# First projections of an RWKV block: seven block products in place of eight

## The reference, cut to what matters

```
h = rms_norm(x, l0_norm)
dx = token_shift(h) - h                 # token t-1 minus token t
x_r, x_w, x_k, x_v, x_a, x_g = (h + dx * mu[i] for i in range(6))
r = x_r @ w_in[:, c[0]:c[1]]            # 1024 x 1024 weights each
k = x_k @ w_in[:, c[1]:c[2]]
v = x_v @ w_in[:, c[2]:c[3]]
g = silu(x_g @ w_in[:, c[3]:c[4]])
w_lo = tanh(x_w @ w_in[:, c[4]:c[5]])   # 64 columns
a_lo = x_a @ w_in[:, c[5]:c[6]]         # 64 columns
kk = k * k_k
```

## Time and profile before

| | us |
|---|---|
| median of 3 runs | 3114.89 (3111.95 to 3125.24) |
| span of the profiled execution | 3120.0 |
| first and last start of a matmul of line 331 | 39.7 and 754.3 |
| matmuls of the projection stage | 3072 |

### The profile page before, as it was taken

One profiled execution on the slowest core, in us unless ns is written; L12 is line 12 of the kernel. 1 busy time (PEld: TensorE's weight loads), 2 busy tenths in 40 slices (PEclk: granted clock), 3 DMA queues, 4 the chain that ended last, 5 costly groups with the idle time before them and its releaser, 6 DMA issues. The chain is left out here.

```text
span 3120.0 us, 78648 instructions
## 1 busy us (share of the span) xinstructions
PE 2897.5 (93%) x35058; PEld 2391.3 (77%) x35058; DVE 1605.3 (51%) x2628; ACT 1080.2 (35%) x2001; POOL 619.7 (20%) x417
## 2 busy tenths in 40 slices
PE   7999999999878888888889999999999999999899
PEld 4887888887467787777777778888777897777677
DVE  5533242433177677677764662222377204777762
ACT  4223332322635445454453441000222113556310
POOL 5522222210023232232321120000000001332320
PEclk9999999999979899899998999999999999999999
DMA  5123331211833232332316763111111226225472
GB/s 173 61 78 115 108 105 48 95 48 53 260 103 112 64 105 77 92 106 70 105 37 179 223 180 74 34 41 41 41 61 61 88 89 229 74 88 181 154 245 85
DMA packets 344272, 326.20 MB, mean 105 GB/s; under 512 B 14159, under 2 KB 258255, under 8 KB 343296
## 3 DMA queue, kind: packets, MB, share of 16 engines
q1 hardware_dynamic: 315344, 261.72, 27.6%
q10 hardware_dynamic: 24480, 47.21, 4.3%
q0 software_dynamic: 4112, 12.25, 1.5%
HBM read 203.18 MB, written 122.64 MB: 104 GB/s over the span
## 5 line engine op out<-in xcount | busy, mean ns | idle before, releaser
L331 PE MATMUL pj_ps<-pj_x_hi,pj_w_hi 128*128 128x512 f32 x1024 | 402.1, 393 | 10.6 <-DVE pj_w_lo L280 5.8
L331 PE MATMUL pj_ps<-pj_x_hi,pj_w_lo 128*128 128x512 f32 x1024 | 399.6, 390 | 0.0
L331 PE MATMUL pj_ps<-pj_x_lo,pj_w_hi 128*128 128x512 f32 x1024 | 399.5, 390 | 0.0
L1924 PE MATMUL dm_ps<-h_hi,dm_w_hi 128*128 128x512 f32 x896 | 279.5, 393 | 0.0
L1924 PE MATMUL dm_ps<-h_lo,dm_w_hi 128*128 128x512 f32 x896 | 275.9, 389 | 0.0
L1924 PE MATMUL dm_ps<-h_hi,dm_w_lo 128*128 128x512 f32 x896 | 275.8, 389 | 0.0
L221 POOL TENSOR_TENSOR pj_x<-h 128x512 f32<-128x512 f32 x128 | 166.7, 1303 | 485.5 <-DVE pj_x_lo L275 436.2
L275 DVE TENSOR_TENSOR pj_x_lo<-pj_x,pj_x_hi 128x512 fp32r<-128x512 f32 x128 | 91.4, 714 | 319.3 <-ACT pj_x_hi L350 319.1
L331 PEld LDWEIGHTS pj_ps<-pj_x_hi,pj_w_hi 128*128 128x128 f32 x1024 | 192.9, 188 | 54.6 <-DVE pj_w_lo L280 8.4
L331 PEld LDWEIGHTS pj_ps<-pj_x_lo,pj_w_hi 128*128 128x128 f32 x1024 | 193.1, 189 | 40.9 <-issue 1.0
L331 PEld LDWEIGHTS pj_ps<-pj_x_hi,pj_w_lo 128*128 128x128 f32 x1024 | 192.8, 188 | 40.4
(11 more groups left out here) (260 smaller groups left out, 6053.9 us busy)
## 6 DMA issues: line engine op xcount, KB each, us to landing
proj<-pj_out ACTq DMA_DIRECT2D x128, 256.0 KB, 2.5
pj_w<-w_in SPq DMA_DIRECT2D x32, 512.0 KB, 4.2
proj<-lr_out SPq DMA_DIRECT2D x32, 512.0 KB, 5.0
dm_w<-w_out SPq DMA_DIRECT2D x32, 512.0 KB, 5.3
dm_w<-w_in SPq DMA_DIRECT2D x32, 512.0 KB, 4.9
partial<-wa_ob SPq DMA_DIRECT2D x48, 264.0 KB, 2.2
mo_part<-partial SPq DMA_DIRECT2D x16, 792.0 KB, 8.6
wa_vt<-v_rows SPq DMA_DIRECT2D x44, 260.0 KB, 3.2
```

Of the source, the lines that this page charges most:

```text
L331: mm = pe.matmul(ps[i][:], wp, xp, start=k == 0 and m == 0, stop=k == KT - 1 and m == len(parts) - 1)
L1924: last = pe.matmul(PS[:, 2 * i + b, :], wp, hp[:, k, t0:t0 + 512], start=k == 0 and m == 0, stop=k == KT - 1 and m == len(parts) - 1)
```

## The change

The 1024 x 1024 by 1024 x 1024 product of each q and each half of the tokens (`u`; 8 groups `g` in all) is done in 2 x 2 blocks of 512 by seven block products (Strassen's scheme in Winograd's form) in place of eight. A block product is four tiles in the code's counting (STEP = 4; `n` counts 224 of them, 28 to a group), and a tile is 12 matmuls of 128 x 512: four banks by three parts. So the stage has 224 x 12 = 2688 matmuls. The order of the products is 1, 2, 7, 6, 5, 4, 3. Product 2 adds on to product 1 in the same four banks, once ACT has copied those banks out, product 6 on to product 7 and product 3 on to product 5.

The scheme needs sums and differences of blocks. POOL makes them of the inputs (`form_x`) and of the weights (`form_w`), 4 operations of 128 x 512 for each of eight forms, and the difference `less_u3` of two outputs; DVE makes the other sums of outputs (`total`), each from a bank and an SBUF tile. Each tile of input and of weights is cast and subtracted anew for each of the 7 products: 224 casts and 224 subtractions of 128 x 512 for each side. 62 of the subtractions of the inputs stand on POOL (`low`, `on_pool`), the others on DVE. The token mix is now ACT's product with `keep` = 1 - mu (`kept`) and a DVE operation (`blend`), with no difference on POOL. The split operands lie in rings of five tiles (DEEP); the work for tile n + 4 waits until tile n - 1 is multiplied. Stores are of 1 MB and issued by SP.

Counts in the stage as the program is built, all operations 128 x 512:

| engine | operations |
|---|---|
| POOL | 256 forms, 62 `x_lo`, 32 `less_u3`, 14 sums of squares: 364 |
| DVE, both inputs in SBUF | 224 `w_lo`, 162 `x_lo`, 128 `blend`, 24 `scale`, 32 `silu`, 7 sums of squares: 577 |
| DVE, one input in PSUM | 128 `total`, 8 `scale` |
| ACT | 448 casts, 128 `kept`, 96 copies from banks and 64 `gate`, 32 squares |

The diff, cut to its core:

```diff
-    PER = 4 * KT
+DEEP = 5
+UNITS = 8
+STEP = HK
+UNIT = 7 * STEP
+ALL = UNITS * UNIT
...
+    def products_of(g):
+        return (1, 2, 7, 6, 5, 4, 3)
...
+    def bank(g, p, j):
+
+        return ps[j + (4 if (p in (1, 2, 5, 3)) == (g % 2 == 0) else 0)]
...
+    def on_pool(n):
+
+        r = (n - 4) % UNIT
+        return n >= 18 and (14 <= r < 18 or 22 <= r < 26)
...
     def gpsimd(pool):
-
-        def difference(k, quarter, n):
-            t0 = quarter * QT
-            if n < 4 * KT:
-                pool.wait_ge(s_normed, n + 1)
-            pool.wait_ge(s_x_lo, n + 1)
-            pool.tensor_tensor(x[k % 2][:], h[:, k, t0:t0 + QT], h[:, k, t0 + 1:t0 + QT + 1],
-                               ALU.subtract).then_inc(s_diff, 1)
...
+            elif p == 5:
+                x_split(pool, g, 1, k)
+                pool.wait_ge(s_tx, tx_at(g, 6, k))
+                made = pool.tensor_tensor(X[0], X[2], X[3], ALU.subtract)
...
+        for n in range(2, ALL):
+            forms(n)
+            for at in prepared(n):
+                if on_pool(at):
+                    low(at)
...
+            g, r = divmod(n, UNIT)
+            if 4 * STEP + 1 <= r < 5 * STEP + 1:
+                less_u3(g, r - 4 * STEP - 1)
...
+        def body(n):
+            total(dve, n)
...
+            for at in prepared(n):
+                if not on_pool(at):
+                    low_x(at)
+                low_w(at)
...
+            if n >= 9 and (at := blended(n - 1)) and at[0]:
+                for name in at[1]:
+                    blend(at[0], name, at[2])
+            silu(dve, n - 2)
...
+            elif p == 2:
+                pe.wait_ge(s_copied, copied_at(g, 1, j))
+            elif p == 6:
+                pe.wait_ge(s_copied, copied_at(g, 7, j))
...
+            for j in range(4):
...
+                parts = product_parts(w_hi[:, at, J], w_lo[:, at, J], x_hi[:, at, :], x_lo[:, at, :])
+                for m, (wp, xp) in enumerate(parts):
+                    first = p not in (2, 6, 3) and k == 0 and m == 0
+                    mm = pe.matmul(bank(g, p, j)[:], wp, xp, start=first, stop=k == HK - 1 and m == len(parts) - 1,
+                                   skip_group_check=True)
...
     def gpsimd(pool):
         before_gpsimd(pool)
-        inputs_read(pool, 3)
+        stored(pool)
         pool.memset(rb[:], NEG).then_inc(s_neg, 1)
...
         before_vector(dve, beside)
+        rings_read(dve)
...
             if b == 0:
+                last_sums(dve)
```

More of the change, by code:

```diff
@@ L133, in projection_buffers @@
[L133 to L141, removed]
@@ L150, in sem @@
     def sem(n):
         return sems.new(f"pj_{n}")
[L153 to L158, removed]
@@ L159, in projection_programs @@
-    s_mm, s_ps_free, s_sig = sem("mm"), sem("ps_free"), sem("sig")
-    s_out, s_scaled = [sem(f"out{i}") for i in range(2)], sem("scaled")
+    s_first = [sem(f"h0{i}") for i in range(HK)]
+    s_block = [[sem(f"h1{i}") for i in range(2)], [sem("h2")], [sem("h3")]]
+    s_ones, s_keep, s_square, s_summed, s_part, s_total, s_log, s_normed = (sem(n) for n in (
+        "ones", "keep", "square", "summed", "part", "total", "log", "normed"))
+    s_y, s_blend, s_tx, s_tw, s_x_hi, s_x_lo, s_x_less, s_w_hi, s_w_lo = (sem(n) for n in (
+        "y", "blend", "tx", "tw", "x_hi", "x_lo", "x_less", "w_hi", "w_lo"))
@@ L347, in scalar @@
[L347 to L357 removed]
+        pool.memset(h[:, :, 0:1], 0.0).then_inc(s_ones, 1)
@@ new lines, in evicts, with body @@
+        def evicts(n):
+            if n < STEP:
+                return
+            g, p, _ = tile_of(n - STEP)
+            k = n % STEP
+            if p not in (1, 7, 2):
+                return
+            if p != 2:
+                tiles = range(4) if k == 0 else ()
+            else:
+                tiles = (2 * k, 2 * k + 1) if k < 2 else ()
+            for j in tiles:
+                evict(g, p, j, n - k)
+        def body(n):
+            evicts(n)
+            if n in (5, 10, 16):
+                inverse_root((5, 10, 16).index(n) + 1)
+            if (at := blended(n)) and not at[0]:
+                for name in at[1]:
+                    kept(0, name, at[2])
+            for at in prepared(n):
+                high_x(at)
+                high_w(at)
+            if (at := blended(n)) and at[0]:
+                for name in at[1]:
+                    kept(at[0], name, at[2])
+            if 4 <= n < 8:
+                square(2, 2 * (n - 4))
+                square(2, 2 * (n - 4) + 1)
+            if 9 <= n < 15:
+                for k in (2 * (n - 9), 2 * (n - 9) + 1) if n < 11 else (n - 7,):
+                    square(3, k)
+            if n >= ALL - 12:
+                beside(n - ALL + 12)
+            gates(act, n - 1)
@@ L447, in low_rank_buffers @@
+    spare = even, other, tiles
+    return (sync, gpsimd, vector, tensor, scalar, last_sums, last_gates, stored, inputs_free, rings_read, banks_read,
+            sums_read, spare)
 def low_rank_buffers(nc, c):
@@ L639, in scalar @@
         sigmoids(NB - 1)
-    spare += [(s_neg, 1), (s_line, len(DILATIONS)), (s_flat, len(DILATIONS)), (s_back, 2)]
-    spare += [(s, 16 * (NB * KT // 4)) for s in s_out]
+    even, other, tiles = spare
+    even = even + [(s, 16 * (NB * KT // 4)) for s in s_out]
+    other = other + [(s_neg, 1), (s_flat, len(DILATIONS))]
+    spare = even + other + tiles
     return sync, gpsimd, vector, tensor, scalar, s_out, s_sig, spare
```

768 lines of the change are left out of this document (531 added, 237 removed).

## The result

| | before | after |
|---|---|---|
| median, us | 3113.42 (4 runs, 3111.18 to 3125.24) | 3200.48 (4 runs, 3199.06 to 3216.78) |
| span of the profiled execution | 3120.0 | 3196.9 |
| projection stage, end of PE's last matmul | 754.7 | 829.7 |
| from there to the end of the span | 2365.3 | 2367.2 |

The ratio is 1.0279, 95% interval 1.0249 to 1.0308. The prediction was 3145 us with a range from 3020 to 3185. The direction and the mechanism came as forecast, the size did not: the stage ends 75 us later than before, where 23 were predicted. What follows it costs 2 us more.

A forecast was written before the change was run, and what follows sets the result against it. DVE (two SBUF inputs) and POOL as one shared resource bound the stage, 87.3 us per group against PE's 76.2. Span 3120 + 23 (stage) + 6 (end) = 3149, 5 above the median: 3145 us, range 3020 to 3185.

The forecast's parts named there:

- PE's pace, 0.2267 us: Projection stage: each matmul takes PE 0.2267 us, so 384 fewer are worth 87 us and a group takes 76.2 us.
- DVE and POOL as one resource: Projection stage: POOL and DVE operations with two SBUF inputs take turns, 87.3 us per group against PE's 76.2; chance 0.53.
- Nothing for the sums from banks: Output sums on DVE with one input in a PSUM bank: priced at nothing in the resource shared with POOL.
- 737 from 37 us on, +4: Projection stage: 737 us of shared DVE and POOL work left at 37 us, PE ending 4 later, at 778: +23.
- Banks: nothing: Product 2 reusing product 1's banks: ACT's last copy is hidden by 9 matmuls, 2.04 us, so it costs nothing.
- The end, +6: Low-rank tables after the stage: fetched behind all stores, 20 us after PE's end, so PE waits some 6 us more.
- PE keeps the pace: First rival, projection stage: DVE and POOL operations pass each other, PE still bounds, median 3016 to 3050 us; chance 0.30.
- The clock: Second rival: PE's pauses lower its clock, matmuls 0.43 us apart for a while, a time of 3180 to 3230; chance 0.12.
- Whole lengths: Third rival: DVE and POOL exclude each other for whole instructions, pairs 1.98 us apart, a time of 3272; chance 0.05.

The follow-up runs named there:

- four doses: Changed kernel with 44, 28, 12 and 0 POOL operations left in a group, the others moved to DVE: medians 3200.48, 3155.19, 3117.82 and 3092.35 us.

## Why the prediction missed

**"PE's pace, 0.2267 us"**: right. With POOL out of the way 28 tiles take 76.2 us, the number of the prediction; so seven products take 76.2 us where eight would take 87.1, as was said. The first matmul started at 24.7 (predicted 24).

**"DVE and POOL as one resource"**: right, and shown by narrowing POOL's tiles, by tiles that nobody reads, and by four doses. Of its prices, those of the shared operations were near: POOL 1.15 against 1.10, a subtraction 0.56 against 0.60, a blend 0.61 against 0.66. In a group these errors give +2.7 and -2.2 us, which nearly cancel by luck.

**"Nothing for the sums from banks"**: this step failed. That a sum does not wait for POOL was read rightly from the earlier trace rows, but the resource was named wrongly: it is DVE's queue, in which a sum takes 0.60 us like any other and is free only as far as it covers a wait. Its 9.6 us less 5.3 hidden are +4.3. The three make the group 92.1 in place of 87.3, some 34 us over seven groups. Since the 5.3 are the remainder of the account, this sum comes out by construction; what measures the term apart from it is the run with narrow sums, 3.2 us a group and a little more for the 0.08 us left of each.

**"737 from 37 us on, +4"**, with no idle time of DVE: this failed too. Busy time of the changed kernel, and DVE's longest waits from 37 to 130 us:

```profile
37.00:60.00 23.00, 14.06 (x49) 10.82 (x48) 14.24 (x15) 14.37 (x26) 13.82 (x10) 0.78 0.23 88
60.00:80.00 20.00, 9.30 (x28) 6.35 (x26) 15.31 (x17) 9.95 (x18) 11.27 (x8) 0.81 0.00 0
80.00:100.00 20.00, 8.37 (x26) 5.82 (x26) 17.09 (x13) 11.03 (x20) 18.66 (x12) 0.67 0.14 53
...
37.00:130.00 93.00, 49.22 (x157) 36.19 (x156) 74.06 (x66) 47.40 (x83) 63.11 (x40) 0.73 0.12 44
...
130.00:800.00 670.00, 585.68 (x2389) 465.37 (x2389) 660.83 (x589) 364.19 (x646) 520.21 (x313) 0.93 0.28 100
```
```profile
DVE pj_x_lo L482 <- ACT pj_x_hi L646: 9.0, 6, 2.2
DVE pj_x L476 <- ACT pj_x L676: 4.9, 2, 2.5
DVE h L467 <- ACT pj_side L708: 2.7, 1, 2.7
```

Of the 93 us from 37 to 130 DVE was idle for 19, the first group's chains (normalise, blend, form, cast, subtract) going from engine to engine, and for 10 more from 130 to the end of PE's work. So from 37 to 829.7 it was busy for 764 us and idle for 29. The forecast had 737 of work and 4 behind it: 27 and 25 make the 52 us by which the stage is longer. That the work grew by 27 and not by the 34 above would fit the first group, where part of POOL's work fell into DVE's idle time and cost nothing. The range had held 4% of idle time, and cheaper prices, but not dearer sums and idle time together.

Whether that idle time is another face of the sharing is seen from the run with narrow tiles of POOL. Here is each kernel from 37 us to its first sum, the changed one and then the narrow one:

```profile
37.00:126.74 89.74, 45.96 (x151) 34.32 (x150) 73.38 (x66) 45.75 (x80) 63.11 (x40) 0.73 0.09 35
```
```profile
37.00:101.97 64.97, 40.91 (x154) 30.77 (x152) 48.31 (x66) 44.22 (x79) 25.88 (x40) 0.82 0.12 46
```

The same 66 operations keep DVE busy for 25 us less, which is what the first sum gains; the idle time stays, 16.4 and 16.7 us. So it does not come from POOL's load. That it comes from the chains is read from the waits and not tested apart.

**"Banks: nothing"**: right. PE's longest waits between 130 and 830 us:

```profile
PE pj_ps L598 <- DVE pj_u L434: 45.7, 18, 5.4
PE pj_ps L598 <- DVE pj_u L442: 20.0, 8, 4.7
...
PE pj_ps L598 <- ACT pj_u L718: 3.0, 3, 1.6
```

The copies that product 2 and product 6 need (L718 is that of product 1) cost 3.0 us there. In the first group, from 37 to 130 us, PE waited once for each of them, 8.9 us for L718 and 3.5 for that of product 7, which is more than nothing; DVE and the clock were not at their steady pace there either, and no run takes these waits apart. The first two rows are a sign that I had not named: I expected PE to wait for `x_lo` and `w_lo`, and it waits mostly for banks whose sums are late in DVE's queue. It is the same lateness; with POOL narrow PE has no wait for a sum between 130 and 690 us, and three for the copies of product 1, 7.8 us in all.

**"The end, +6"**: +1.9. The end of the stage, and the tables (before: the earlier trace rows):

```profile
829.31 0.39 PE L598 MATMUL pj_ps<-pj_x_hi,pj_w_lo 128*128 128x512 f32 x1
830.58 0.47 PE L964 MATMUL lr_down<-lr_h_hi,lr_w_hi 128*128 128x512 f32 x1 [0.88 <-DVE lr_h_low L946]
...
848.91 1.43 PE L987 MATMUL lr_up<-lr_hot,lr_rb 33*8 33x383 f32 x2 [6.92 <-DMA lr_hot<-onehot]
```

The tables are multiplied 19.6 us after the last matmul's start (predicted 20), with PE waiting 6.9 us; but the span grew by 1.9 only, so some of that wait is made good later, and no run shows where.

**Rivals.** PE keeps the pace: no, the engines don't pass each other. The clock: its grant was 0.93 in the steady stretches shown, with PE's pauses, and 0.98 to 1.00 in the same places with POOL narrow, where the pauses were nearly gone; I count nothing for it there, since DVE was busy for 99 of 100 us while it was low. In the first group it was 0.73 and DVE was idle for a fifth of the time, so what the clock cost there stays open. Whole lengths: pairs start 1.70 us apart, not 1.98. The Trainium skill (SBUF — State Buffer, SBUF: two separate sides) gives whichever of the two starts first the pair for the whole instruction; the rows give 1.10 of POOL's 1.29 us and 0.60 of DVE's 0.69. Another rule of the Trainium skill (SBUF — State Buffer, Who interferes with whom) is that a VectorE instruction with at most one SBUF input, outside the 2-port perf modes, does not contend with GpSimd. The trace bears it out: 0.68 us for each sum, beside a busy POOL too.

## What to carry to other kernels

Before work is put on POOL because it looks free, count what it takes from DVE: here 1.10 us of DVE's queue for each 128 x 512 operation of two SBUF tiles, where DVE does the same work in 0.60, so POOL helps only where DVE would be idle. A cost that "doesn't wait" still has its place in an in-order queue, and whether it is hidden depends on what runs beside it at that place; moving that cover away can cost what the move saves. When an accounting of the steady part comes near the bound, add the start-up, where engines hand single tiles to each other, as a term of its own.

## What the runs showed of the hardware that I had not expected

DVE and POOL take strict turns when both always have work: ten operations of DVE on end start 1.70 us apart, from 470.25 to 485.55, in the stretch shown in part, and neither engine is starved. The time for which an operation keeps the other engine out is less than its printed length (1.10 of 1.29 us, 0.60 of 0.69); on DVE the next one is seen to begin before the last one has ended (431.90, against 431.30 and 0.67). And a change of engine for 44 of a group's 124 operations moved the same program by 108 us (3200.48 to 3092.35) without one operation less.
